# One-core decoder trunk in FP32 parts: work moved off VectorE's queue, an earlier x, wo groups dealt anew, a last expert slot by halves

## Chip, cores and metric

One core of one Trainium2 chip. The metric is the device time of one execution in microseconds; the time before is the median of three runs. A view of the profile shows one profiled execution, with times from its first instruction.

## The reference, cut to what matters

x is 256 tokens by 1024 features, float32. The trunk has two layers, each a mixer and a channel mixer, with an RMS norm ahead of each and a plain residual add behind it.

```python
for i in range(DEPTH):                       # DEPTH = 2
    u = rms_norm(h, norm_mix[i])
    mix = diff_attention(u, ...) if i == 0 else moba_attention(u, ...)   # w_qkv 1024x3072, w_o 1024x1024
    h = h + mix
    u = rms_norm(h, norm_ffn[i])
    ffn = swiglu(u, ...) if i == 0 else moe_swiglu(u, ...)               # d_ff 2816; 8 experts of 3584, top 2
    h = h + ffn
return rms_norm(h, final_norm)
```

## The kernel before, in words

Every weight passes through one pipeline. A **slot** is a weight tile of 2 MB (`ring`, seven of them); a **group** is 128x512 of it, eight to a slot. SyncE (SP) loads a slot when the slot seven ahead of it is used up. ScalarE (ACT) copies two groups at a time into `whi` (twelve groups deep, line 508, in the experts line 681): the rounded high part. VectorE (DVE) subtracts it from the slot and leaves the low part in `wlo` (line 863, two or four groups at a time; line 1123 in the experts). TensorE (PE) multiplies three times for each product: high by high, high by low, low by high (lines 1312 to 1314). Activations are split in the same way into `xhi` (ACT, line 528) and `xlo` (DVE, line 871). All order is written out by hand in four instruction streams; `split_to(n)` on ACT and `halve_to(n)` on DVE work through the groups up to n (rounded up to the piece: one group in the first slot, four in whole slots of the dense FFN, two elsewhere), and an engine that waits in one of them does nothing else.

**Start.** x comes as two halves of 128 tokens (`rowbuf`), PE turns both (line 1476), ACT and DVE split them, and PE runs slot 0. The first slot comes in pieces (`head_in`, line 450). `keep_clock` (line 1465) issues transposes whose result nobody reads; 16 stand at the start and 10 ahead of the first gather. The norm's scale isn't applied to x: squares are summed (`squares` line 518, `add_squares` line 896), PE sums columns after the second group of slot 1 (`sum_norm`, line 1337) and spreads the result after the fifth (`spread_norm`, line 1342), and q, k, v are scaled when they leave PSUM.

**Attention steps.** Each layer has 16 units (pair of heads by token block) and 18 steps. In step t PE does scores(t), weigh_values(t-2) (line 1458), the first part of FILL[t] projection groups, turn_probs(t-1) (line 1442) and the rest. The groups of FILL are what PE has to do while ACT and DVE work on the softmax. Per step DVE does `minima`, `combine` (layer 0), its halving up to 8 + FILL[t]//2 groups ahead, then `output_rows(t-2)`, then more halving; ACT does `exps`, its splitting, `copy_probT`. FILL ends the 32 qkv groups at step 10; the two slots of wo (16 groups) follow, 6 of them in steps 13 to 17. After step 11 PE turns heads 0 to 3 (line 1327), after step 16 heads 4 and 5, after the steps the last two (`turn_heads(3, 4)`). In layer 0 the turn waits for `norm_heads` (DVE line 989), which waits for GpSimd (POOL, line 814), which waits for ACT's `head_square` and that for `output_rows`. wo sums over k (features) into two halves of the output: psA is half 0, psB half 1. The second wo slot of layer 0 goes two k of half 0, two of half 1, and again; that of layer 1 goes half 0 whole, then half 1 with four groups woven (lines 1532 to 1539).

**Dense FFN.** It starts as soon as the residual add (line 890) has been split again. PE sums the norm in the first up slot, after its groups 1 and 5 (lines 1519 to 1522); DVE can scale the gate product only then.

**Router, then experts.** After wo of layer 1 DVE adds the residual (lines 890, 1162) and splits the rows (`raw_lo`, line 1128), PE makes the logits (line 1551), a chain of small steps chooses experts and gathers rows (line 1585). The expert loop runs 8 times (`extra` more are possible), 21 slots each. Down slots go by k with both halves in turn. At its end `yhi` (ACT, line 764) and `ylo` (DVE, line 1293) scale the result for the scatter, which stands in the next iteration or, behind the last one, at line 1675.

Of the kernel before, what the change touches and what calls it, by code (L numbers as in the profile page):

```python
# [26 lines left out]
ALU = mybir.AluOpType  # L27
# [3 lines left out]
P = 128  # L31
GROUP = 512
# [8 lines left out]
def trunk(nc, x, norm_mix, norm_ffn, diff_w_qkv, diff_w_o, diff_lambda, diff_subln, moba_w_qkv, moba_w_o,  # L41
# [64 lines left out]
    FILL = [3] * 10 + [2, 0, 0, 2, 1, 1, 1, 1]  # L106
# [7 lines left out]
    assert sum(FILL) == 4 * GS + 6  # L114
# [25 lines left out]
    with ExitStack() as ctx:  # L140
# [28 lines left out]
        halfneg = sb("halfneg", [P, 2 * PAIRS])  # L169
        score_min = sb("score_min", [P, 2, UNITS, 2])  # L170
# [84 lines left out]
        consts = sem("consts")  # L255
        gains_T = sem("gains_T")
# [111 lines left out]
        def half_and_k(s, g):  # L368
            if s == first_slot["wo", 0] + 1:
                return g // 2 % 2, g // 4 * 2 + g % 2  # L370
            return divmod(g, slots[s][1] // 2)

        def part_of(t, s, g, size=1):
# [6 lines left out]
            return slot[:, g * GROUP:(g + size) * GROUP].rearrange("p (g n) -> p g n", n=GROUP)  # L380

# [52 lines left out]
        def _(sp):  # L434
            sp.dma_start(rowbuf[:, 0, :], x[0, 0:P, :]).then_inc(x_in[0], 16)
            for s, (src, groups) in enumerate(slots):
# [6 lines left out]
                if s in paired:  # L443
                    dst = dst.rearrange("p (k a n) -> p k a n", a=2, n=T)
                    first = 0
                    if s == 0:
                        for j in range(3):
                            ks = slice(2 * j, 2 * j + 2)
# [45 lines left out]
        def _(act):  # L494
# [98 lines left out]
            act.dma_start(rowbuf[:, 1, :], x[0, P:T, :]).then_inc(x_in[1], 16)  # L593
            split_to(1)
            act.wait_ge(gains_set, 1)
            for q in range(KD // 2):
                normed_hi(0, q)
                split_to(2 * q + 3)
# [76 lines left out]
            def item_split(i, first, last):  # L675
                for m in range(first, last, 2):
# [4 lines left out]
                    nc.scalar.copy(hi_of(NG + m, 2), part_of(ring, NS + j, g, 2)).then_inc(hi_done, 2)  # L681
# [60 lines left out]
            with act.Fori(0, n) as i:  # L742
# [19 lines left out]
                for half in range(2):  # L762
                    act.wait_ge(group_used, used_at(i, IG - 1 + half))
# [11 lines left out]
        def _(pool):  # L775
# [28 lines left out]

            def root(norm, at):
# [13 lines left out]
            nc.gpsimd.memset(f(ylo[:, :]), 0.0).then_inc(ylo_done, 2)  # L819
            root(3, rstd[:, 0, :])  # L820
# [26 lines left out]
        def _(dve):  # L847
# [144 lines left out]
            for layer in range(2):  # L992
                for pair in range(PAIRS):
                    for i in range(2):
                        nc.vector.memset(q_scale[64 * i:64 * i + 64, layer, pair:pair + 1],
                                         -SCALE / slopes[layer][2 * pair + i])
# [5 lines left out]
            halve_to(1)  # L1002
            for q in range(KD // 2):
                normed_lo(0, q)
                halve_to(2 * q + 3)
            for layer in range(2):
# [7 lines left out]
                norm_spread(2 * layer)  # L1014
                copy_qk(layer, 0)
# [51 lines left out]
                halve_to(end - 2 + AHEAD)  # L1067
# [5 lines left out]
                halve_to(end + AHEAD - 2)  # L1073
# [7 lines left out]
                halve_to(first_group[up_slot[0] + 1])  # L1081
                norm_column(1)
                norm_diagonals(1)
                halve_to(first_group[up_slot[0] + 1] + 4)
# [613 lines left out]
```

## Time and profile before

| what | value |
| --- | --- |
| median of 3 runs | 1527.39 us (1523.25 to 1528.58) |
| profiled execution, own time | 1523.65 us |
| its span | 1521.7 us |
| PE busy | 1480.4 us, 97% |
| DVE, ACT busy | 1183.8 us, 1003.2 us |
| expert loop | from 476.1 us to 1508.8 us, about 129 us an iteration |

The own time is the span and 1.95 us around it. Idle time stands in brackets ahead of an instruction, with what ended it. PE's busy time hides that its clock may be halved; the windows give that as PEclk (1.00 is 2.4 GHz, 0.50 is 1.2 GHz).

### The profile page before, as it was taken

What the parts mean: (1) busy time and instruction counts of PE and PEld (TensorE: products, weight loads), DVE (VectorE), ACT (ScalarE), POOL (GpSimd) and SP (SyncE); (2) the same over time, 40 slices, a digit from 0 to 9 for tenths busy, and PEclk for the clock granted to TensorE, in tenths of its full rate; (3) what the DMA queues carried; (4) which work ended last, traced back from release to release, by engine and by line L of the source; (5) the groups of instructions that cost most, each with busy time, mean ns of one, the idle gap of its engine ahead of it and who ended that gap; (6) DMA issues with size and microseconds to landing.
All of it is one profiled execution on the core that took longest, in us unless ns stands there. A gap on an engine that the chain in (4) does not pass through costs nothing.

```text
span 1521.7 us, 23192 instructions
## 1 busy us (share of the span) xinstructions
PE 1480.4 (97%) x8172; PEld 1257.6 (83%) x8172; DVE 1183.8 (78%) x1176; ACT 1003.2 (66%) x1322; POOL 22.1 (1%) x50
## 2 busy tenths in 40 slices
PE   8989999999999999999999999999999999999997
PEld 8878999999887878777887787878778787778875
DVE  6776555566558888888888888888888888888887
ACT  5555444446547776777777777777777777767775
POOL 0000000000001000000000000000000000000000
PEclk9989999999999999999999999999999999999998
DMA  9833444474324999999899999989989999998981
GB/s 336 305 112 111 167 167 141 164 271 170 114 106 161 345 360 327 331 361 360 303 351 364 330 322 360 339 308 366 360 311 345 360 327 331 359 362 302 354 305 42
DMA packets 187543, 426.36 MB, mean 280 GB/s; under 512 B 4641, under 2 KB 23234, under 8 KB 187458
## 3 DMA queue, kind: packets, MB, share of 16 engines
q1 hardware_dynamic: 187104, 424.33, 77.6%
q10 hardware_dynamic: 354, 1.07, 0.2%
q8 instruction: 33, 0.54, 0.1%
q14 instruction: 52, 0.43, 0.1%
HBM read 424.33 MB, written 1.05 MB: 280 GB/s over the span
## 4 chain that ended last, share of the span: by engine, by line
PE 83%; DVE 7%; ACT 4%; issue 4%; DMA 0%; ACTq 0%; DVEq 0%; POOL 0%; POOLq 0%
PE psA L1312 9%; PE psA L1314 9%; PE psA L1313 9%; PE psB L1312 9%; PE psB L1314 9%; PE psB L1313 9%; PE psY L1312 8%; PE psY L1314 7%; PE psY L1313 7%; DVE wlo L1123 3%; PE psY L1585 2%; ACT whi L681 2%; PE psB L1612 2%; PE psY L1458 1%; DVE wlo L863 1%
## 5 line engine op out<-in xcount | busy, mean ns | idle before, releaser
L1123 DVE TENSOR_TENSOR wlo<-ring,whi 128x2048 fp32r<-128x2048 f32 x339 | 761.4, 2281 | 131.6 <-ACT whi L681 128.7
L681 ACT CAST whi<-ring 128x1024 fp32r<-128x1024 f32 x676 | 678.7, 1054 | 133.9 <-PE psY L1314 65.6
L863 DVE TENSOR_TENSOR wlo<-ring,whi 128x1024 fp32r<-128x1024 f32 (+2 forms) x104 | 152.7, 1488 | 69.4 <-ACT whi L508 68.8
L1312 PE MATMUL psB<-whi,ihi 128*128 128x512 f32 x448 | 181.6, 405 | 6.9 <-DVE wlo L1123 6.9
L1312 PE MATMUL psY<-whi,hhi 128*128 128x512 f32 x448 | 182.7, 408 | 0.0
L1312 PE MATMUL psA<-whi,ihi 128*128 128x512 f32 x448 | 177.8, 397 | 3.4 <-DVE ilo L1214 2.1
L1314 PE MATMUL psA<-whi,ilo 128*128 128x512 f32 x448 | 177.2, 396 | 0.0
L1314 PE MATMUL psB<-whi,ilo 128*128 128x512 f32 x448 | 177.1, 395 | 0.0
L1313 PE MATMUL psA<-wlo,ihi 128*128 128x512 f32 x448 | 176.9, 395 | 0.0
L1313 PE MATMUL psB<-wlo,ihi 128*128 128x512 f32 x448 | 176.9, 395 | 0.0
L1314 PE MATMUL psY<-whi,hlo 128*128 128x512 f32 x448 | 176.9, 395 | 0.0
L1313 PE MATMUL psY<-wlo,hhi 128*128 128x512 f32 x448 | 176.9, 395 | 0.0
L508 ACT CAST whi<-ring 128x1024 fp32r<-128x1024 f32 (+1 forms) x134 | 133.3, 1022 | 63.9 <-PE psY L1314 27.5
L1312 PE MATMUL psA<-xhi,whi 128*128 128x256 f32 x368 | 108.2, 294 | 4.0 <-DVE xlo L871 2.5
L693 ACT CAST hhi<-psB 128x512 fp32r<-128x512 f32 x56 | 32.9, 587 | 119.4 <-PE psB L1612 119.4
L1312 PEld LDWEIGHTS psY<-whi,hhi 128*128 128x128 f32 x448 | 84.5, 189 | 28.9 <-DVE wlo L1123 12.0
L1312 PE MATMUL psB<-xhi,whi 128*128 128x256 f32 x368 | 107.2, 291 | 0.0
L1312 PEld LDWEIGHTS psB<-whi,ihi 128*128 128x128 f32 x448 | 84.4, 188 | 27.2 <-DVE wlo L1123 9.9
L1312 PEld LDWEIGHTS psA<-whi,ihi 128*128 128x128 f32 x448 | 84.4, 188 | 26.4 <-DVE wlo L1123 4.8
L1313 PE MATMUL psA<-xlo,whi 128*128 128x256 f32 x368 | 105.9, 288 | 0.0
L1314 PE MATMUL psA<-xhi,wlo 128*128 128x256 f32 x368 | 105.9, 288 | 0.0
L1314 PE MATMUL psB<-xhi,wlo 128*128 128x256 f32 x368 | 104.5, 284 | 0.0
(277 smaller groups left out, 2294.6 us busy)
## 6 DMA issues: line engine op xcount, KB each, us to landing
ring<-in_moe_w_gate SPq DMA_DIRECT2D x57, 2048.0 KB, 7.8
ring<-in_moe_w_up SPq DMA_DIRECT2D x56, 2048.0 KB, 7.8
ring<-in_moe_w_down SPq DMA_DIRECT2D x56, 2048.0 KB, 7.7
ring<-in_ffn_w_gate SPq DMA_DIRECT2D x5, 2048.0 KB, 9.0
ring<-in_ffn_w_up SPq DMA_DIRECT2D x5, 2048.0 KB, 8.2
ring<-in_ffn_w_down SPq DMA_DIRECT2D x5, 2048.0 KB, 7.9
ring<-in_moba_w_qkv SPq DMA_DIRECT2D x8, 1024.0 KB, 7.5
ring<-in_diff_w_qkv SPq DMA_DIRECT2D x6, 1024.0 KB, 12.2
```

The source lines that it names most:

```text
L508: nc.scalar.copy(hi_of(m, size), part_of(ring, s, g, size)).then_inc(hi_done, size)
L681: nc.scalar.copy(hi_of(NG + m, 2), part_of(ring, NS + j, g, 2)).then_inc(hi_done, 2)
L693: nc.scalar.copy(hhi[:, :, place_of(c)], psB[:, 1, :].rearrange("p (b t) -> p b t", t=P)).then_inc(m_hhi, 1)
L863: nc.vector.tensor_tensor(part_of(wlo, s, g, size), part_of(ring, s, g, size), f(hi_of(m, size)), ALU.subtract).then_inc(lo_done, size)
L1123: nc.vector.tensor_tensor(part_of(wlo, NS + j, g, step), part_of(ring, NS + j, g, step), f(hi_of(NG + m, step)), ALU.subtract).then_inc(lo ...
L1312: mm(ps, xh, wh, start=start, stop=False, skip_group_check=shared)
L1313: mm(ps, xh, wl, start=False, stop=False, skip_group_check=shared)
L1314: return mm(ps, xl, wh, start=False, stop=stop, skip_group_check=shared)
L1458: ins = mm(psY[:, 3, i * wide:(i + 1) * wide], probsT[:, u % 2, i * (tb + 1) + kb, :], val[:, kb, c:c + wide], start=kb == 0, stop=kb == tb)
L1585: ins = mm(psY[:, 2 + q, (k % 4) * P:(k % 4 + 1) * P], rows_[:, tb * D + k * P:tb * D + (k + 1) * P], pick[:, tb, :], start=part == 0 and ...
L1612: ins = nc.tensor.transpose(psB[:, 1, fb * P:(fb + 1) * P], hid[:, fb * P:(fb + 1) * P], ident[:, :])
```

## The change

- x's second half is issued by SP behind the first two pieces of slot 0, no longer by ACT behind the gains. ACT and DVE split one group more ahead of each part of x. `keep_clock` adds 4 transposes behind the first half of x and 10 behind the second.
- 32 memsets of q_scale leave DVE; POOL makes q_scale (16 memsets and three operations). Five small operations ahead of the router leave DVE for POOL. DVE waits for `scales_set` in three places.
- FILL for steps 11 to 17 becomes 0, 2, 2, 2, 1, 1, 3: 11 groups of wo in place of 6. `turn_heads(3, 4)` stands right behind the steps; five groups follow it in both layers. The second wo slot of layer 1 is laid like that of layer 0.
- Between the layers' halves DVE halves less ahead of the residual add; the norm of the FFN is summed after group 0 of the up slot and spread after group 3.
- The last slot of an expert runs all k of half 0, then of half 1; `yhi` of half 0 waits for four groups less.

```diff
@@ -103,7 +103,7 @@
 STEPS = UNITS + 2
-FILL = [3] * 10 + [2, 0, 0, 2, 1, 1, 1, 1]
+FILL = [3] * 10 + [2, 0, 2, 2, 2, 1, 1, 3]
...
@@ -111,7 +111,7 @@
 assert all(filled[layer][11] == first_group[first_slot["wo", layer]] for layer in range(2))
-assert sum(FILL) == 4 * GS + 6
+assert sum(FILL) == 4 * GS + 11
...
@@ -167,6 +167,7 @@
     halfneg = sb("halfneg", [P, 2 * PAIRS])
+    second_head = sb("second_head", [P, 1])
...
@@ -253,6 +254,7 @@
     consts = sem("consts")
+    scales_set = sem("scales_set")
...
@@ -366,7 +368,7 @@
     def half_and_k(s, g):
-if s == first_slot["wo", 0] + 1:
+if s in (first_slot["wo", 0] + 1, first_slot["wo", 1] + 1):
...
@@ -378,6 +380,12 @@
+    def item_part(t, j, g, size):
+if j == IS - 1:
+    half, k = divmod(g, FBW)
+    return t[(NS + j) % RING][:, :].rearrange("p (k h n) -> p h k n", h=2, n=GROUP)[:, half, k:k + size, :]
+return part_of(t, NS + j, g, size)
...
@@ -445,6 +453,8 @@
             for j in range(3):
+                if j == 1:
+                    sp.dma_start(rowbuf[:, 1, :], x[0, P:T, :]).then_inc(x_in[1], 16)
...
@@ -590,12 +600,11 @@
 act.dma_start(gain_rows[4 * KD:4 * KD + 1, :], diff_subln[:, :]).then_inc(gains_in, 16)
-act.dma_start(rowbuf[:, 1, :], x[0, P:T, :]).then_inc(x_in[1], 16)
-split_to(1)
+split_to(2)
     normed_hi(0, q)
-    split_to(2 * q + 3)
+    split_to(2 * q + 4)
...
@@ -678,7 +687,7 @@
         act.wait_ge(group_used, used_at(i, m + 2 - HL))
-        nc.scalar.copy(hi_of(NG + m, 2), part_of(ring, NS + j, g, 2)).then_inc(hi_done, 2)
+        nc.scalar.copy(hi_of(NG + m, 2), item_part(ring, j, g, 2)).then_inc(hi_done, 2)
...
@@ -760,7 +769,7 @@
     for half in range(2):
-        act.wait_ge(group_used, used_at(i, IG - 1 + half))
+        act.wait_ge(group_used, used_at(i, IG - 4 + 4 * half))
...
@@ -801,6 +810,15 @@
+pool.wait_ge(consts, 1)
+for pair in range(PAIRS):
+    nc.gpsimd.memset(q_scale[:, 0, pair:pair + 1], -SCALE / slopes[0][2 * pair])
+    nc.gpsimd.memset(q_scale[:, 1, pair:pair + 1], -SCALE / slopes[1][2 * pair])
+link(nc.gpsimd.memset(second_head[:, :], 1.0))
+link(select(second_head[:, :], slopes[1][0] / slopes[1][1], ALU.is_gt, 64, [[0, 1]], -1))
+nc.gpsimd.tensor_tensor(q_scale[:, 1, :], q_scale[:, 1, :], repeat(second_head[:, 0], 1, PAIRS),
+                        ALU.mult).then_inc(scales_set, 1)
...
@@ -817,6 +835,12 @@
 nc.gpsimd.memset(f(ylo[:, :]), 0.0).then_inc(ylo_done, 2)
+nc.gpsimd.memset(over[:, 0:5], 0.0)
+nc.gpsimd.memset(over2[:, 0:2], 0.0)
+nc.gpsimd.memset(over4[:, 0:4], 0.0)
+nc.gpsimd.tensor_scalar(first_place[:, :], expert_no[:, :], float(P), None, ALU.mult)
+nc.gpsimd.tensor_scalar(jump_base[:, :], expert_no[:, :], -float(P), float(P * (E - 1)), ALU.mult,
+                        ALU.add).then_inc(scales_set, 1)
...
@@ -989,20 +1013,15 @@
 
-for layer in range(2):
-    for pair in range(PAIRS):
-        for i in range(2):
-            nc.vector.memset(q_scale[64 * i:64 * i + 64, layer, pair:pair + 1],
-                             -SCALE / slopes[layer][2 * pair + i])
 dve.wait_ge(gains_set, 1)
-halve_to(1)
+halve_to(2)
     normed_lo(0, q)
-    halve_to(2 * q + 3)
+    halve_to(2 * q + 4)
...
@@ -1012,6 +1031,7 @@
     norm_spread(2 * layer)
+    dve.wait_ge(scales_set, 1)
...
@@ -1064,13 +1084,12 @@
         break
-    halve_to(end - 2 + AHEAD)
+    halve_to(end + 4)
         normed_lo(2, q)
-    halve_to(end + AHEAD - 2)
...
@@ -1078,10 +1097,10 @@
     sum_squares(1)
-    halve_to(first_group[up_slot[0] + 1])
+    halve_to(first_group[up_slot[0]] + 4)
     norm_diagonals(1)
-    halve_to(first_group[up_slot[0] + 1] + 4)
+    halve_to(first_group[up_slot[0] + 1])
...
@@ -1120,7 +1139,7 @@
         dve.wait_ge(hi_done, used_at(i, m + step))
-        nc.vector.tensor_tensor(part_of(wlo, NS + j, g, step), part_of(ring, NS + j, g, step),
+        nc.vector.tensor_tensor(item_part(wlo, j, g, step), item_part(ring, j, g, step),
...
@@ -1140,14 +1159,9 @@
                         ALU.subtract).then_inc(rt_split, 1)
-nc.vector.tensor_scalar(first_place[:, :], expert_no[:, :], float(P), None, ALU.mult)
-nc.vector.tensor_scalar(jump_base[:, :], expert_no[:, :], -float(P), float(P * (E - 1)), ALU.mult, ALU.add)
-nc.vector.memset(over[:, 0:5], 0.0)
-nc.vector.memset(over2[:, 0:2], 0.0)
-link(nc.vector.memset(over4[:, 0:4], 0.0))
 
-dve.wait_ge(group_used, NG - 4)
+dve.wait_ge(group_used, NG - 2)
...
@@ -1181,6 +1195,7 @@
 norm_column(3)
+dve.wait_ge(scales_set, 2)
...
@@ -1477,6 +1492,7 @@
             ins.then_inc(turn_done, 1)
+    keep_clock(10 if tb else 4)
...
@@ -1500,8 +1516,7 @@
     end = first_group[first_slot["wo", layer] + 2]
-    last_turn = end - GS + (2 if layer == 0 else 0)
-    fill(layer, filled[layer][STEPS], last_turn)
+    last_turn = filled[layer][STEPS]
...
@@ -1516,9 +1531,9 @@
                 turned_group(up_slot[c], g, 2, psB, width[c])
-                if c == 0 and g == 1:
+                if c == 0 and g == 0:
                     sum_norm(1)
-                if c == 0 and g == 5:
+                if c == 0 and g == 3:
...
@@ -1527,16 +1542,15 @@
 
-fill(1, last_turn, end - 4)
+fill(1, last_turn, end - 2)
 for fb in range(4):
-    for k in range(4):
-        pe.wait_ge(xlo_done, 4 * ATTN[1] + 2 + k // 2 + 1)
-        ins = rows_block(end - 4 + k, fb, block_of(1, fb), xhi[:, 4 + k, :], xlo[:, 4 + k, :], False, k == 3)
+    for k in range(2):
+        ins = rows_block(end - 2 + k, fb, block_of(1, fb), xhi[:, 6 + k, :], xlo[:, 6 + k, :], False, k == 1)
     if fb == 3:
-        ins.then_inc(group_used, 4)
+        ins.then_inc(group_used, 2)
...
@@ -1620,7 +1634,7 @@
         m = GS * j + g
-        wh, wl = whi_of(NG + m), part_of(wlo, NS + j, g)[:, 0, :]
+        wh, wl = whi_of(NG + m), item_part(wlo, j, g, 1)[:, 0, :]
...
@@ -1631,7 +1645,7 @@
         if kind == "down":
-            k, half = divmod(g, 2)
+            half, k = divmod(g, FBW) if j == IS - 1 else (g % 2, g // 2)
...
```

## Rows read from the trace of the kernel before

**Rows 1.** The page: the span, and the first line of the busy times.

```profile
span 1521.7 us, 23192 instructions
...
PE 1480.4 (97%) x8172; PEld 1257.6 (83%) x8172; DVE 1183.8 (78%) x1176; ACT 1003.2 (66%) x1322; POOL 22.1 (1%) x50
```

**Rows 2.** Windows: us, busy PE, PEld, DVE, ACT, POOL (instructions), PEclk, DMA, GB/s.

```profile
10.14:16.97 6.83, 6.15 (x29) 6.18 (x30) 6.83 (x15) 5.43 (x13) 0.00 (x0) 0.50 1.06 376
...
98.90:102.31 3.41, 1.28 (x9) 0.85 (x8) 3.33 (x12) 2.64 (x9) 0.00 (x0) 1.00 0.84 265
102.31:112.55 10.24, 8.28 (x38) 6.95 (x39) 7.10 (x23) 5.21 (x16) 0.00 (x0) 0.50 0.29 117
...
122.78:126.20 3.42, 3.42 (x20) 3.41 (x18) 0.09 (x1) 1.34 (x3) 0.00 (x0) 0.50 0.00 0
126.20:142.70 16.50, 16.50 (x138) 16.29 (x137) 10.49 (x11) 7.45 (x13) 1.20 (x2) 1.00 0.37 128
```

**Rows 3.** Timeline of PE, start: start us, us, instruction, count, idle before.

```profile
8.38 1.09 PE L1476 MATMUL psY<-ident,rowbuf 128*128 128x128 f32 x8 [1.11 <-DMA rowbuf<-in_x]
10.82 0.55 PE L1312 MATMUL psA<-xhi,whi 128*128 128x256 f32 x1 [1.34 <-DVE xlo L871]
...
28.22 0.47 PE L1312 MATMUL psB<-whi,xhi 128*128 128x512 f32 x1
```

**Rows 4.** Timelines of the other engines, start.

```profile
0.83 3.08 DVE L995 MEMSET q_scale<- 64x1 f32 x32 [0.83 <-PEq L1689]
1.21 3.15 SPq L450 DMA_DIRECT2D ring<-in_diff_w_qkv  x6
...
2.28 0.36 ACTq L593 DMA_DIRECT2D rowbuf<-in_x  x1
...
18.07 1.05 ACT L508 CAST whi<-ring 128x1024 fp32r<-128x1024 f32 x1 [2.50 <-DMA ring<-in_diff_w_qkv]
19.02 2.04 ACT L601 COPY resT<-psY 128x512 f32<-128x512 f32 x4
...
26.11 3.49 DVE L863 TENSOR_TENSOR wlo<-ring,whi 128x1024 fp32r<-128x1024 f32 x3
```

**Rows 5.** Timeline of PE, layer 0: steps 11 to 16, dense FFN's start.

```profile
101.52 0.33 PE L1442 MATMUL psY<-ident,probs 128*128 128x128 f32 x1 [2.11 <-DVE probs L964]
...
106.90 0.69 PE L1442 MATMUL psY<-ident,probs 128*128 128x128 f32 x2 [0.83 <-DVE probs L964]
...
120.83 0.33 PE L1442 MATMUL psY<-ident,probs 128*128 128x128 f32 x1 [1.62 <-DVE probs L964]
121.86 0.46 PE L1458 MATMUL psY<-val,probsT 128*128 128x128 f32 x2 [0.69 <-DVE rowbuf L977]
...
143.88 0.36 PE L1312 MATMUL psA<-xhi,whi 128*128 128x256 f32 x1 [1.18 <-DVE xlo L871]
...
175.22 0.39 PE L1312 MATMUL psA<-xhi,whi 128*128 128x256 f32 x1 [1.44 <-DVE wlo L863]
```

**Rows 6.** Timeline of DVE, layer 0, steps 12 and 17 and the wo groups.

```profile
106.77 1.40 DVE L882 SCALAR_TENSOR_TENSOR xlo<-psA,gain_cols,xhi 128x512 fp32r<-128x512 f32 x2
...
130.27 0.76 DVE L989 TENSOR_TENSOR rowbuf<-rowbuf,head_rstd 128x256 f32<-128x256 f32 x2 [1.84 <-POOL head_rstd L814]
...
136.78 4.50 DVE L863 TENSOR_TENSOR wlo<-ring,whi 128x2048 fp32r<-128x2048 f32 x2 [1.20 <-ACT whi L508]
```

**Rows 7.** Waits, 413 to 450 us (layer 1): total, times, longest.

```profile
PE psY L1458 <- ACT probsT L561: 1.5, 2, 1.2
```

**Rows 8.** Timeline of DVE behind wo of layer 1.

```profile
456.14 1.29 DVE L890 TENSOR_TENSOR resT<-psA,resT 128x512 f32<-128x512 f32 x2 [0.18 <-PE psA L1314]
...
462.83 0.76 DVE L1128 TENSOR_TENSOR ilo<-resT,ihi 128x256 fp32r<-128x256 f32 x2
```

**Rows 9.** Waits of PE over the whole span: total, times, longest.

```profile
PE psB L1312 <- DVE wlo L1123: 6.9, 7, 1.4
```

**Rows 10.** The chain, at an expert iteration's end: start us, us, what.

```profile
604.44 2.64 issue
```

**Rows 11.** Timeline of PE behind the last expert.

```profile
1510.74 0.50 PE L1675 MATMUL psY<-yhi,pickT 128*128 128x512 f32 x1 [1.94 <-DVE ylo L1293]
```

## The prediction, made before the changed kernel was run

> **What bounds the kernel now.** I read the page first: PE is busy for 97% of the span [rows 1], so a part of the change counts only where PE waits, or where its clock is low. The windows come next, for the clock [rows 2]. It is at 0.50 (1.2 GHz) from 10.14 to 16.97, from 102.31 to 112.55 and from 122.78 to 126.20: 20.5 us, of which half, 10.2 us, would come back at 2.4 GHz if PE had work throughout. The timelines of PE show its waits: 1.11 and 1.34 us at the start [rows 3], 2.11, 0.83, 1.62 and 0.69 in steps 11 to 16 of layer 0, 1.18 ahead of the dense FFN and 1.44 in it [rows 5]. In the expert loop seven waits sum to 6.9 us [rows 9]. What ends nearly all of them is DVE, in the order its stream is written in, often behind a copy by ACT. So each part is judged by where it puts things in DVE's order.
>
> A group is 12 matmuls; at full clock 138 matmuls took 16.50 us [rows 2], 0.12 us each, so a group takes 1.43 us. A copy of two groups by ACT takes 1.05 us, a halving of two by DVE 1.2 us (3.49 for three) [rows 4], one of four 2.25 us (4.50 for two) [rows 6].
>
> **Costed at nothing.** The 32 memsets run from 0.83 to 3.91 [rows 4], and DVE's next work waits for gains that PE turns well after that; POOL is idle then, and the scales are wanted only after 30 us. DVE's five small operations ahead of the router sit in time that it waits for ACT anyway. If that cover were gone they would cost about 0.5 us. SP issues x at its third place: 1.21 plus two issues of 0.53 is 2.27, ACT issued it at 2.28 [rows 4]. So it isn't issued sooner; it only stands ahead of the later pieces of slot 0 in one queue. The last slot by halves: ACT gets `yhi` of half 0 earlier, but `ylo` stands behind DVE's halving for the next item, in the loop and at the end, so PE's wait of 1.94 us [rows 11] stays.
>
> **Start.** x may land between as late as now and 1.11 us sooner, where PE's wait for it ends [rows 3]. I take 0.7, nearer to the latter since x moves ahead of 1.5 MB of weights. The extra transposes fill the 1.34 us wait, so the clock should stay up: slot 0 starts at 10.2 and ends after 96 x 0.12 = 11.5 us, at 21.8; two groups of slot 1 take it to 24.6. That is over 3 us ahead, but it doesn't last. The third group needs a halving that stands behind the sum of squares on DVE: it starts at 26.11 and the first of its three pieces ends at 27.3 [rows 4]. That chain hangs on ACT, which can copy x (19.02) only after slot 1 has landed (18.07) [rows 4]; nothing here lands it sooner. So PE resumes at 27.3 where it was at 28.22 [rows 3]: **0.9 us gained**, with some 2.3 us of new idle time ahead. The clock fell behind waits of 2.11 and of 1.62 + 0.69 [rows 2, 5]; behind 1.18 and 1.44 [rows 5] no fall is seen. The new one is nearest to the first two, so I take a fall, 3.4 us long as the shortest was [rows 2], that costs 1.7: **+0.8 us**; bounds -0.9 and +0.8.
>
> **Layer 0, steps 12 to 17.** FILL gives PE work in steps 12 to 14, but each group has to be split first.
> - Step 12: PE is free at 106.07 (106.90 less 0.83 [rows 5]). Its next instruction is now the first wo group, which needs `xlo` of heads 0 to 3; DVE makes it until 108.17 [rows 6]. The softmax work that ran at 106.90 is queued behind that. Wait 2.1.
> - Steps 13 to 15: halvings now stand ahead of `output_rows`; I get waits of 0.1, 0.05 and 0.4.
> - Step 16: the halving of the last wo pair (1.2) stands ahead of `combine`, as in the case of the 1.62 wait: 1.35.
> - Step 17: its first group belongs to heads 4 and 5, turned just before: 0.9.
> - `turn_heads(3, 4)`: halving up to 9 groups ahead now reaches into the FFN, where pieces are four wide. So two copies (2.1) and a halving of four (2.25) stand ahead of `output_rows` of the last unit (0.35); from there to the end of `norm_heads` it was 2.6 (130.27 - 1.84 to 131.03 [rows 6]). With 0.4 for ACT to get there that is 7.7 us, against 0.9 and three groups, 5.2: wait 2.5. Before, five groups covered it.
>
> New waits 7.4, old ones 0.83 + 1.62 + 0.69 = 3.1: +4.3. The half clock from 122.78 goes (-1.7), and in that up to 112.55 PE has some 1.2 us less work (-0.6): **+2.0**. The last wait (2.5) is nearest to 2.11, so another fall: +1.7. Together **+3.7**; bounds: -3 (old waits go, nothing new) and +5.
>
> **Dense FFN.** The halving of four that stood ahead of the residual add moves behind it, so the wait of 1.18 goes. But there it is in front of the squares. I get 0.35 at gate group 4 and 1.2 at the first up group, whose halving follows the sum of squares: **+0.4**; bounds -1.2 and +2.25 (the whole piece uncovered). The spread comes two groups sooner, but the wait of 1.44 [rows 5] starts with PE's end of the up slot: no change.
>
> **Layer 1, steps.** No POOL chain here, and no pieces of four. Step 12 waits 1.3 for the heads, later waits (1.5 in one group [rows 7]) shrink by as much: **0**, bounds -1.5 and +1.3, with +1.7 if the clock falls.
>
> **Behind wo of layer 1.** The new layout finishes psA two groups before the end, not four. DVE's chain from psA to the last split rows took from 456.14 to 463.59, 7.45 us, nearly all busy [rows 8]. Four groups covered 5.7 of it, two cover 2.9: **+2.9**. Bounds: +1.6 (DVE's own waits for ACT inside it, 1.3, vanish) and +4.
>
> **Sum.** 0.8 + 3.7 + 0.4 + 0 + 2.9 = +7.8. On the profiled execution's own 1523.65 (span 1521.7 and 1.95 around it) that is 1531.4. It lies 3.7 below the median of the runs, 1527.39, near their fastest. For a median of new runs I take the middle between 1531.4 and 1535.2: **1533.5 us**. About 0.3% (4.6 us) is what a measurement of this kernel can tell from no change.
>
> **Rivals.**
> - *The waits are covered* (0.27). PE reaches the new groups later than I reckon, the clock stays up: -0.9 at the start, 0 in layer 0, 0.4 in the FFN, 2.9 behind wo: +2.4, some 1528. For it: half of my waits in layer 0 are under 1 us, the size of my error. Against: the 2.1 of step 12 and the 2.5 of the last turn are orders in the code.
> - *The clock* (0.10), the one that ends faster. The extra transposes and groups keep 2.4 GHz through all three stretches: -10.2, and the 2.9 behind wo stays: -7.3, 1520. It decides at two points: slot 1 mustn't wait for the squares (they would have to end by 24.6), and the wait of 2.11 in step 11, ahead of the fall at 102.31, would have to go; no group is added ahead of it.
> - *The code of the expert loop* (0.06). At an iteration's end ACT stands still for 2.64 us in "issue" [rows 10], with nothing to wait for, and then PE waits for a halving that waits for ACT; the seven waits are 6.9 us [rows 9]. DVE's and ACT's streams ahead of the loop get shorter; if that moved the code so that ACT's stop went, the sum would be +0.9, some 1528.5. Against: only one ACT instruction goes. The Trainium skill ("Runtime: NRT & Kernel Launch", Instruction fetch mechanics) says that a taken branch to a page of code that is no longer held has to wait for it to be fetched; by that rule DVE, whose code does shift, could gain such a stop as well as ACT lose one. The trace agrees in that the stop stands right at ACT's loop end.
> - *A part that doesn't do what it says*: the last slot by halves, in all cases at zero, for the reason above.
>
> **How the numbers follow.** My forecast has 0.57, its own range 1530 to 1537. Faster: the clock, 0.10. Within 0.3%: covered waits and code, 0.33. Slower: 0.57. The range takes in the covered waits (1528 less 3 for the spread of runs) and, above, a fall in layer 1 (+1.7) and one behind wo (+1): 1525 to 1539.
>
> **What would show it.** Right: slot 1's third group waits for DVE near 24.6 to 27.3 and the clock is 0.50 right behind; in layer 0 PE waits about 2 us for `xlo` ahead of the first wo group and 2.5 ahead of the last turn; from PE's last wo group to the last row split it is 4.6 us, not 1.8. Wrong: if the last turn doesn't wait, or if PE's waits per expert iteration (about 1 us) change, in either direction; the second would outweigh all else here.

## The result, and the profile after

The changed kernel takes **1538.05 us** (median of 4 runs, 1537.45 to 1540.89), the kernel before beside it 1526.63: ratio **1.0081**, 95% interval 1.0058 to 1.0103: slower by 11.4 us in the medians, by 12.4 in the ratio. The prediction was 1533.5 with 1525 to 1539, and slower as the likeliest case; the measured time lies 1 us inside the upper end. The profiled execution is the slowest of the four (1540.89); so its span lies 17.4 us over that of before [rows 1], while the medians lie 11.4 apart. The page of the changed kernel begins:

```profile
span 1539.1 us, 23210 instructions
...
PE 1490.5 (97%) x8186; PEld 1260.6 (82%) x8186; DVE 1182.6 (77%) x1139; ACT 1002.7 (65%) x1322; POOL 23.4 (2%) x74
```

PE is busy 10 us longer though its program is nearly the same. The busy share says nothing about it; the clock in the windows does (us, busy PE, PEld, DVE, ACT, POOL with instructions, PEclk, DMA, GB/s):

```profile
10.00:14.00 4.00, 3.75 (x31) 3.69 (x31) 4.00 (x9) 4.00 (x11) 0.00 (x0) 1.00 1.07 375
...
29.43:32.85 3.42, 3.42 (x10) 2.64 (x9) 2.58 (x6) 2.38 (x3) 0.72 (x1) 0.50 1.06 381
...
104.53:114.77 10.24, 6.94 (x32) 6.23 (x33) 5.36 (x15) 4.07 (x12) 0.00 (x0) 0.50 0.29 116
...
473.17:483.00 9.83, 9.83 (x50) 9.37 (x47) 5.82 (x27) 6.71 (x10) 3.50 (x10) 0.50 0.10 35
483.00:493.65 10.65, 10.65 (x38) 9.39 (x38) 7.18 (x21) 6.57 (x15) 2.65 (x6) 0.50 0.01 2
```

Slot 0 now runs at 2.4 GHz from its start, and the falls of before at 10.14 and 122.78 [rows 2] are gone. In their place stand 3.41 us at 29.43 and 20.48 us, from 473.17 to 493.65, where before had none. The timeline of PE shows what stands ahead of each, and PE's other waits (start us, us, instruction, count, idle before):

```profile
27.38 0.61 PE L1352 MATMUL psY<-ones,hidT 128*128 128x1 f32 x4 [2.54 <-DVE hidT L926]
28.52 0.50 PE L1327 MATMUL psB<-whi,xhi 128*128 128x512 f32 x1 [0.53 <-DVE wlo L887]
...
110.50 0.55 PE L1327 MATMUL psA<-xhi,whi 128*128 128x256 f32 x1 [2.25 <-DVE xlo L906]
...
130.40 0.44 PE L1457 MATMUL psY<-ident,probs 128*128 128x128 f32 x2 [1.12 <-DVE probs L988]
132.93 0.36 PE L1327 MATMUL psA<-xhi,whi 128*128 128x256 f32 x1 [0.92 <-DVE xlo L906]
...
139.48 0.66 PE L1342 MATMUL psY<-ident,rowbuf 128*128 128x128 f32 x4 [2.01 <-DVE rowbuf L1013]
...
153.81 0.38 PE L1327 MATMUL psA<-xhi,whi 128*128 128x256 f32 x1 [0.18 <-DVE wlo L887]
160.87 0.39 PE L1327 MATMUL psB<-xhi,whi 128*128 128x256 f32 x1 [1.06 <-DVE wlo L887]
...
471.09 0.29 PE L1565 MATMUL psA<-ihi,rt_parts 128*16 128x256 f32 x1 [2.44 <-DVE ilo L1147]
...
472.32 0.29 PE L1565 MATMUL psA<-ihi,rt_parts 128*16 128x256 f32 x1 [0.59 <-DVE ilo L1147]
...
1528.21 0.50 PE L1689 MATMUL psY<-yhi,pickT 128*128 128x512 f32 x1 [1.92 <-DVE ylo L1308]
```

These are the orders that the prediction read out of DVE's stream: the sum of squares ahead of the third group of slot 1, the heads ahead of the first wo group (2.25, [rows 5] had 0.83 there), `norm_heads` ahead of the last turn (2.01), the split rows ahead of the logits (2.44 and 0.59), and `ylo` at the end as before (1.92, [rows 11]). The 1.18 ahead of the FFN [rows 5] is gone.

Landmarks by stage, from the traces of all kernels (us; the fifth number is from the last logits product to the end of the first expert iteration; "half" is how long the clock was at 0.50, leaving out the tail behind the experts). The kernels of the lower part are told below.

| kernel | scores(0) | to first FFN down | layer 1: scores(0) to logits | logits | to end of iteration 1 | half |
| --- | --- | --- | --- | --- | --- | --- |
| before | 39.9 | 152.7 | 99.4 | 2.1 | 136.2 | 20.5 |
| changed | 41.9 | 156.2 | 100.3 | 5.3 | 142.1 | 34.1 |
| changed, second trace | 43.3 | 156.4 | 102.8 | 5.4 | 138.1 | 37.6 |
| changed_tile_last | 42.6 | 156.4 | 100.4 | 5.3 | 139.4 | 27.3 |
| logits_filled | 41.0 | 155.9 | 100.3 | 5.3 | 136.4 | 13.7 |
| start_only | 41.9 | 152.7 | 99.1 | 2.1 | 138.7 | 23.9 |
| start_x_on_act | 43.5 | 151.7 | 102.2 | 2.1 | 137.8 | 27.3 |
| fill_layer0_only | 38.8 | 154.8 | 102.4 | 2.1 | 137.9 | 27.3 |
| l1_tail_only | 38.4 | 152.9 | 99.3 | 5.0 | 139.0 | 23.9 |
| one_tile_more | 39.1 | 151.7 | 102.4 | 2.1 | 138.1 | 23.9 |
| parts_left | 38.9 | 153.3 | 99.4 | 2.1 | 136.2 | 13.7 |
| squares_ahead_of_slot1 | 37.4 | 152.2 | 102.4 | 2.1 | 137.8 | 23.9 |
| filled_waits | 37.2 | 151.6 | 99.4 | 2.1 | 137.7 | 10.2 |
| filled_waits_2 | 38.0 | 148.7 | 99.3 | 2.1 | 136.3 | 0 |

### The profile page after: what moved, and what is told of

The parts are those of the page before. It is cut to its first block, busy times and chain, and to the rows that moved or that the text cites. A ratio compares the mean times of both kernels' runs of the same rounds, so it can differ in the third digit from the quotient of the medians.

```text
span 1539.1 us, 23210 instructions
## 1 busy us (share of the span) xinstructions
PE 1490.5 (97%) x8186; PEld 1260.6 (82%) x8186; DVE 1182.6 (77%) x1139; ACT 1002.7 (65%) x1322; POOL 23.4 (2%) x74
## 4 chain that ended last, share of the span: by engine, by line
PE 81%; DVE 7%; ACT 5%; issue 5%; DMA 1%; SPq 0%; ACTq 0%; POOL 0%; DVEq 0%; POOLq 0%
PE psB L1327 9%; PE psA L1327 9%; PE psB L1329 9%; PE psB L1328 9%; PE psA L1329 8%; PE psA L1328 8%; PE psY L1327 7%; PE psY L1329 7%; PE psY L1328 7%; DVE wlo L1142 3%; PE psY L1599 2%; ACT whi L690 2%; PE psB L1626 2%; DVE wlo L887 1%; ACT whi L518 1%
## 5 line engine op out<-in xcount | busy, mean ns | idle before, releaser
L690 ACT CAST whi<-ring 128x1024 fp32r<-128x1024 f32 x676 | 678.5, 1054 | 136.4 <-PE psY L1329 66.2
L887 DVE TENSOR_TENSOR wlo<-ring,whi 128x1024 fp32r<-128x1024 f32 (+2 forms) x104 | 152.9, 1489 | 66.3 <-ACT whi L518 65.9
L1328 PE MATMUL psB<-xlo,whi 128*128 128x256 f32 x368 | 104.0, 283 | 0.0
```

The source lines that it names most:

```text
L690: nc.scalar.copy(hi_of(NG + m, 2), item_part(ring, j, g, 2)).then_inc(hi_done, 2)
L887: nc.vector.tensor_tensor(part_of(wlo, s, g, size), part_of(ring, s, g, size), f(hi_of(m, size)), ALU.subtract).then_inc(lo_done, size)
L1328: mm(ps, xh, wl, start=False, stop=False, skip_group_check=shared)
```

## The experiments

Some of the kernels have one part of the change each, some the whole change with one thing altered, and some are new versions of the kernel before. There are eleven, and the changed kernel ran a second time; the twelve ran on four chips, each beside the kernel before (medians 1525.18 to 1527.19).

**The changed kernel again,** for a second trace. I expected 1537 to 1539, with a fall of the clock of 10 to 20 us behind the logits. Measured: 1537.70 against 1525.18, ratio 1.0078 (1.0063 to 1.0093). Behind the logits the clock was at 0.50 for 3.41 and 6.83 us (from 475.09 and 485.33). It was also at 0.50 for 6.83 in layer 1's steps and 3.41 in the experts, where the first trace had none.

**The end of wo of layer 1 alone.**

```diff
-            if s == first_slot["wo", 0] + 1:
+            if s in (first_slot["wo", 0] + 1, first_slot["wo", 1] + 1):
...
-            dve.wait_ge(group_used, NG - 4)
+            dve.wait_ge(group_used, NG - 2)
...
-            fill(1, last_turn, end - 4)
+            fill(1, last_turn, end - 2)
```

> The kernel before with only the new end of wo of layer 1: its second slot is laid two k of half 0, two of half 1, and again, DVE adds the residual from two groups before the end (not four), and the merged loop has two k. In the trace of the changed kernel the clock is at 0.50 from 473.17 to 493.65, behind waits of 2.44 and 0.59 us in the logits. Theory: the layout alone makes this wait and the fall. Then PE waits 2 to 3 us in the logits, the clock is 0.50 for 13 to 21 us behind it, the experts' first group comes 8 to 12 us later than before, and the time is 1535 to 1539 us. Rival (the fall needs what lies ahead of it, the other waits of layer 1): the wait is there, but no fall, and the time is +2.9, 1529 to 1531.

Measured: 1528.94 against 1526.11, ratio 1.0025 (1.0014 to 1.0035). The wait is there, and behind it a fall. Timeline of PE, then windows:

```profile
463.69 0.29 PE L1550 MATMUL psA<-ihi,rt_parts 128*16 128x256 f32 x1 [2.23 <-DVE ilo L1128]
464.93 0.29 PE L1550 MATMUL psA<-ihi,rt_parts 128*16 128x256 f32 x1 [0.59 <-DVE ilo L1128]
```

```profile
467.00:473.50 6.50, 5.43 (x49) 5.08 (x48) 4.98 (x23) 6.34 (x9) 3.72 (x10) 1.00 0.09 33
473.50:483.74 10.24, 9.48 (x31) 8.04 (x31) 8.09 (x22) 7.10 (x15) 2.63 (x6) 0.50 0.01 2
```

The logits take 5.0 us in place of 2.1: +2.9, the number of the prediction. But the clock stays up for 8.6 us behind the wait and falls then, in the gathers. Both theories have a half: the price of the wait is the rival's, the fall is my theory's, though not where it put it, and the time (+2.8) is just under what both had.

**The logits' wait filled, in the changed kernel.**

```diff
             for k in range(KD):
+                if k in (4, 6):
+                    keep_clock(20 if k == 4 else 4, psY[:, 3, T + P:2 * T])
                 pe.wait_ge(tlo_done, k + 1)
```

> The kernel after with 20 transposes that nobody reads ahead of PE's wait for the fifth logits block and 4 ahead of the seventh, in a bank that is free there. They take about 0.12 us each at full clock, 2.4 + 0.5, as much as the waits of 2.44 and 0.59. Theory: the half clock from 473.17 to 493.65 comes from these idle times; it goes, and with it 7 to 10 us: 1528 to 1531. Rival: the clock is set by how little PE does in the chain of small steps behind the logits as well; then it falls all the same, within 10 us behind the logits, and the time is 1536 to 1538.

Measured: 1534.45, ratio 1.0066 (1.0040 to 1.0092) against the same kernel before. The transposes take the place of the wait, and the clock is 1.00 through the logits, the chooser and the gathers:

```profile
467.40 2.34 PE L1480 MATMUL psY<-ident 128*128 128x128 f32 x20
470.00 0.29 PE L1567 MATMUL psA<-ihi,rt_parts 128*16 128x256 f32 x1 [0.25 <-DVE ilo L1147]
```

```profile
472.00:480.00 8.00, 6.91 (x60) 6.30 (x58) 6.31 (x27) 6.70 (x10) 3.87 (x11) 1.00 0.14 51
480.00:490.00 10.00, 8.18 (x43) 6.71 (x42) 8.63 (x22) 8.00 (x16) 2.22 (x5) 1.00 0.00 0
```

From the last logits product to the end of the first iteration it is 136.4 us, against 142.1, 138.1 and 139.4 in the three traces of the change with the wait: 1.7 to 5.7 us less, not the 7 to 10 that I expected from the one trace I had. In the medians it is 3.6, in the ratios 0.12 to 0.15%, with intervals that overlap.

**FILL and the last turn in layer 0 alone.**

```diff
-    FILL = [3] * 10 + [2, 0, 0, 2, 1, 1, 1, 1]
+    FILL = [[3] * 10 + [2, 0, 2, 2, 2, 1, 1, 3], [3] * 10 + [2, 0, 0, 2, 1, 1, 1, 1]]
...
-                last_turn = end - GS + (2 if layer == 0 else 0)
+                last_turn = end - GS if layer else filled[layer][STEPS]
```

> The kernel before with the new FILL (0, 2, 2, 2, 1, 1, 3 from step 11) and the new place of the last turn in layer 0 alone. The prediction had +2.0 for the waits, and +1.7 for a fall of the clock behind the last turn. The trace of the changed kernel has no fall there. Theory: from before scores(0) to the first down group of the FFN it is +1.5 to +3, of which most lies at the last turn (a wait of about 2 us), and the time is 1528 to 1531. Rival: with the other parts of the change away, the clock falls behind the last turn as I had assumed: +3.7.

Measured: 1529.44, ratio 1.0021 (1.0012 to 1.0031). From scores(0) to the first down group 154.8 us, +2.1. PE's waits:

```profile
107.10 0.55 PE L1311 MATMUL psA<-xhi,whi 128*128 128x256 f32 x1 [2.25 <-DVE xlo L881]
...
127.52 0.44 PE L1441 MATMUL psY<-ident,probs 128*128 128x128 f32 x2 [1.10 <-DVE probs L963]
130.05 0.55 PE L1311 MATMUL psA<-xhi,whi 128*128 128x256 f32 x1 [0.92 <-DVE xlo L881]
136.60 0.66 PE L1326 MATMUL psY<-ident,rowbuf 128*128 128x128 f32 x4 [0.69 <-DVE rowbuf L988]
```

Here the clock was at 0.50 from 129.62 to 133.03, ahead of the last turn and not behind it. PE came later to a wait whose end DVE sets, and so waited 0.69 and not 2.01: here a fall ahead of a wait cost less than half its length, since the wait took most of it up. The rival's fall behind the last turn was in none of the five traces with this FILL.

**The start alone,** and with x on ACT's queue again.

```diff
+                            if j == 1:
+                                sp.dma_start(rowbuf[:, 1, :], x[0, P:T, :]).then_inc(x_in[1], 16)
...
-                split_to(2 * q + 3)
+                split_to(2 * q + 4)
...
+                keep_clock(10 if tb else 4)
```

> The kernel before with only the changed start: x's second half issued by SP, one group more split ahead of each part of x, 4 and 10 more transposes. Theory: slot 0 runs at full clock from about 10.3, the third group of slot 1 waits about 2.5 us for DVE, the clock falls to 0.50 behind that for 3.4 us, and scores(0) comes between +0.8 (my sum) and +2.0 (what the changed kernel's trace shows) later than before; 1528 to 1530. Rival: the +2.0 of the changed kernel comes from the POOL operations or the wait on them, which are away here; then scores(0) is within 0.5 us of the place of before.

> The changed start alone, but x's second half is issued by ACT as before. With the whole new start, slot 1's landing let ACT go on at 19.25, with first group at 10.37; in a kernel with the old start at 17.37, with first group at 10.17. Theory: x in SP's queue, ahead of five pieces of the weights, pushes the landing of slot 1 back by 1 to 1.9 us, and with it the squares and the third group of slot 1. With x back on ACT slot 1 lands as before, the wait for the squares is 0.6 to 1.3 us in place of 2.55, and scores(0) comes 1 to 2 us sooner than with the new start, at 39.9 to 40.9. Rival: the landing differs between executions whatever the queue; then it stays near 19 and scores(0) at 41.9.

Measured: 1527.65, ratio 1.0016 (1.0003 to 1.0028), scores(0) at 41.9; with x on ACT 1525.19, ratio 1.0000 (0.9990 to 1.0010), scores(0) at 43.5. My theory of the queue fell in the trace: slot 1 lands late with x on either queue (timeline of ACT, x on ACT; [rows 4] had 18.07):

```profile
19.61 1.05 ACT L508 CAST whi<-ring 128x1024 fp32r<-128x1024 f32 x1 [4.32 <-DMA ring<-in_diff_w_qkv]
```

That trace is of the slowest of its kernel's ten runs (1529.71), so it may overstate the cost. Whether x on SP costs anything, the two overlapping intervals leave open.

**The squares ahead of slot 1,** an order of my own on the kernel before.

```diff
-                split_to(2 * q + 3)
+                split_to(min(2 * q + 3, GS))
...
                     squares(3 * layer, q)
+                    if layer == 0 and q == 1:
+                        split_to(GS + 2)
```

> The kernel before with another order at the start: ACT copies x and squares half of it before it splits the first two groups of slot 1, DVE adds the first square before it halves them. The chain to the sum of squares no longer starts with the landing of slot 1. Theory: PE's waits ahead of the third group of slot 1 (0.9 to 2.5 us in all the traces so far) go, the third group starts at 2.9 us from the end of slot 0, and scores(0) comes 1 to 1.5 us sooner than with the order of before: 37 to 38.7; total -1. Rival: ACT's split of slot 1's first groups comes later than PE wants it, and what is won in front of the third group is lost in front of the first.

DVE's side is cut in the same way (halving to 8, and of two more behind the first add). Measured: 1524.83 against 1525.18, ratio 0.9997 (0.9987 to 1.0006). PE doesn't wait ahead of the third group of slot 1, which starts at 25.7 (28.2 before, [rows 3]), and scores(0) comes at 37.4, 2.5 us sooner than in the trace of before and 1.0 to 1.6 sooner than in the other traces with the old start. The total doesn't show it: in this trace the clock fell at 426.27 and at 477.47 for 10.2 us together, where the trace of before had none.

**One tile more, unused.** Outside PE's waits, an expert iteration took 128.34 and 128.35 us in the changed kernel's and `logits_filled`'s traces, and 128.05 to 128.08 in those of the seven kernels without the whole change that had run by then.

```diff
         halfneg = sb("halfneg", [P, 2 * PAIRS])
+        unused = sb("unused", [P, 1])
```

> The kernel before with one tile more, a single number per partition, unused, declared where the change declares second_head. Three traces with the whole change have PE's expert iterations at 128.35 us without their waits, seven traces without it at 128.05 to 128.08, and the difference is spread over the whole iteration. The new tile moves all tiles behind it by 32 bytes in each partition (ihi from 205056 to 205088, hhi, hlo, ilo, q_hi, k_hi with it), so that they no longer begin at a multiple of 64. Theory: that slows PE's reading of them; then this kernel has 128.3 to 128.4 per iteration without waits, and 2 to 3 us more in all, 1527.5 to 1529 beside 1525 to 1526. Rival: it is the code or the order of the last slot; then it is 128.05 to 128.08 and the time that of before.

> The whole change, but second_head is declared behind all other tiles, so that it moves none; nothing else differs. Before with one tile more had 128.33 us per expert iteration without waits, the parts left with second_head last 128.04. Theory: the iterations come to 128.05, the total 2 to 3 us under the changed kernel's, 1534.5 to 1536 where before is at 1525 to 1526.5; the waits (2.25 ahead of the first wo group, 2.0 at the last turn, 2.44 in the logits) stay, with a fall of 3 to 20 us behind the last. Rival: in the changed kernel the 0.28 per iteration has another cause as well, then it stays above 128.2.

Measured: `one_tile_more` 1527.13, ratio 1.0007 (0.9997 to 1.0017); the change with `second_head` as the last tile 1538.71 against 1527.19, ratio 1.0076 (1.0063 to 1.0089). The totals don't tell it, the traces do. Windows over iterations 3 to 8: before, one tile more, changed, changed with the tile last:

```profile
729.14:1504.53 775.39, 768.49 (x3494) 619.52 (x3494) 660.64 (x451) 567.22 (x648) 0.00 (x0) 1.00 0.91 330
```

```profile
732.20:1509.72 777.52, 770.02 (x3494) 617.79 (x3494) 660.69 (x451) 567.33 (x648) 0.00 (x0) 1.00 0.91 329
```

```profile
745.00:1522.00 777.00, 770.00 (x3494) 617.81 (x3493) 660.91 (x451) 566.49 (x648) 0.00 (x0) 1.00 0.90 329
```

```profile
743.09:1518.56 775.47, 768.41 (x3494) 618.93 (x3494) 660.90 (x451) 566.60 (x648) 0.00 (x0) 1.00 0.91 330
```

The same 3494 matmuls at the same clock keep PE busy for 768.49 and 768.41 us where the tiles begin as before, and for 770.02 and 770.00 where one tile of a number has pushed them by 32 bytes. That is 1.5 us in six iterations, 2 in eight. In iteration length without waits it is 128.33 with the tile and 128.06 in the change without its push. Both kernels differ from their partner in nothing but that tile. The other traces agree: in iterations 3 to 8 the mean without waits is 128.33 to 128.35 in all four traces where the tile pushes the others, and 128.04 to 128.09 in the other ten.

**The parts left:** operations from DVE to POOL, the FFN's orders, the last slot by halves, on the kernel before, with `second_head` last.

```diff
-                halve_to(end - 2 + AHEAD)
+                halve_to(end + 4)
...
-                        k, half = divmod(g, 2)
+                        half, k = divmod(g, FBW) if j == IS - 1 else (g % 2, g // 2)
```

> The parts of the change not tried so far, on the kernel before: the operations moved from DVE to POOL, the FFN's new orders, the last slot by halves; with second_head declared behind all other tiles, so that it moves none. Layer 1's end, FILL and the start are as before. Theory: each is worth little. Expert iterations 128.05 to 128.08 us without waits; the wait of 1.18 ahead of the FFN goes and 1.2 comes at the first up group, so the first down group is within 0.6 of before, counted from scores(12); PE's last wait stays 1.94; the total within 1 us of before. Rival: the iterations are at 128.35 as in the changed kernel, so the last slot or the code is the cause and not the tile's place; then +2 to 3 us.

Measured: 1526.80, ratio 1.0007 (0.9996 to 1.0018). scores(12) to the first down group +0.4, iterations 128.04 without waits, the last wait 1.94.

**Waits filled with transposes,** on the kernel before, first and second version. Both also have the squares ahead of slot 1, and the change's 4 and 10 transposes behind x. The cut shows the second; the first has {11: 16, 12: 6, 16: 12} and nothing in layer 1.

```diff
+                        if layer == 0:
+                            keep_clock({11: 18, 12: 4, 15: 13}.get(t, 0), psY[:, 2, T + P:2 * T])
                         turn_probs(layer, t - 1)
...
+                    if layer == 1 and t == 12:
+                        pe.wait_ge(qk_raw, 2 * (4 * layer + 3) + 2)
+                        keep_clock(9)
                     if t < UNITS:
                         scores(layer, t)
```

> The kernel before with that order of the start, the 4 and 10 transposes behind x, 16, 6 and 12 transposes ahead of the turns of probabilities in steps 11, 12 and 16 of layer 0 (in the bank that these turns use), and 16 ahead of the last scatter. Nothing else of the change. Theory: the clock falls behind idle time of PE of about 2 us and stays up where transposes run in its place; then the half clock of before (6.83, 10.24 and 3.41 us in layer 0, and some of the tail) goes, and the time is 10 to 12 us less: 1514 to 1517. Rival: the clock goes by how much PE does in the steps with no groups; then it falls in steps 11 to 14 all the same, the gain is 2 to 4 us, and the time is 1522 to 1524.

> The kernel with filled waits, with the transposes better placed: 18 in step 11 and 4 in step 12 ahead of the turns of probabilities, 9 ahead of the turn of heads in step 11, 13 in step 15 (12 stood in step 16, too late for the wait of 1.62), in layer 1 nine ahead of scores(12), 18 in place of 10 ahead of the first gather, 16 ahead of the experts. Its first trace still had falls of 3.41 us at 117.10 and 6.83 at 468.67. Theory: both go, and those that other traces show at 427 to 437, and the time is 2 to 5 us under that of the kernel with filled waits: 1516 to 1519. Rival: transposes also put work behind them late; then the falls go and the time stays at 1521.

Measured: 1521.16 against 1525.18, ratio **0.9977** (0.9968 to 0.9986), then 1518.20 against 1526.23, ratio **0.9954** (0.9940 to 0.9969). Of the first, its rival's time came nearer than mine (4 us gained, 10 to 12 expected): the fall of step 11 was gone, but one at 117.10 stayed behind a wait of 1.62, where I had the step wrong by one, and one at 468.67. In the second the clock is at 1.00 from 10.68, where its record begins in this trace, to 1509.13, where PE has all but finished:

```profile
10.68:500.00 489.32, 478.17 (x3698) 450.35 (x3697) 318.48 (x549) 262.48 (x469) 16.43 (x28) 1.00 0.52 182
500.00:1509.00 1009.00, 998.34 (x4546) 804.06 (x4544) 859.00 (x590) 737.85 (x850) 1.00 (x3) 1.00 0.91 330
1509.13:1515.50 6.37, 0.00 (x0) 0.00 (x0) 2.54 (x2) 0.00 (x0) 1.79 (x3) 0.50 0.41 165
```

It beats both kernels. Its six runs lie within 3 us (1517.3 to 1520.3), the 23 of before on the same chip within 6.7.

## Why the prediction was right, and where it was not

**The direction and the range held;** the sum was +7.8, measured +11.4. (The middle of 1531.4 and 1535.2 is 1533.3, not 1533.5; and by that same middle the rival on code would be at 1526.4 and the clock at 1518.2, where I gave 1528.5 and 1520.) The parts, each alone, give in ratios 16 (start), 21 (layer 0), 25 (behind wo of layer 1), 7 (the tile) and 7 (the parts left) hundredths of a per cent: 0.76%, 11.6 us, about what was measured (0.76 to 0.81% in three comparisons). Each single ratio has an interval of 1.5 to 2 us either way, and layer 1's new FILL, +1.0 in the traces, ran in none of them, so that the sum fits so well is partly luck. The parts as read from traces come to some 15 us, more than the medians show; the gap is open, though in both measurements of the changed kernel the profiled execution was the slowest of four.

- *Start, forecast +0.8.* Right in kind: 2.54 us for DVE's squares, the clock at 0.50 for 3.41 from 2 us behind that wait, slot 0 at full clock. The term that failed is the 0.9 us gained: the third group starts at 28.52, 0.3 later than the 28.22 of before, not at 27.3. With the 1.7 of the half clock, as I had it, that is the +2.0 of this trace. In the trace of before scores(0) is at 39.9; the four others with the old start have 38.4 to 39.1, the six with the new one 41.0 to 43.5. So traces show about +3.4, totals +2.4 (1.0016) and 0 (x on ACT). Two things were missing: the half clock at 10.14, which is part of why before reached its third group only at 28.22, is 6.83 us in that trace and 0 to 3.41 in the others; and "nothing here lands it sooner" should have allowed for later: slot 1's last packet lands at 18.3 to 19.5, at 17.3 to 18.1 in the eight kernels that don't split one group further.
- *Layer 0 and FFN, forecast +3.7 and +0.4.* Measured 3.2 to 3.8 from scores(0) to the first down group. The waits came nearly as worked out (forecast 2.1, 1.35, 0.9, 2.5, FFN 0.35 and 1.2; measured 2.25, 1.12, 0.92, 2.01, 0.18, 1.06). The fall that I had assumed behind the last turn (+1.7) never came, and still the total was nearly met: that is luck. What it made up for is that the clock gave back less than the 2.3 us of the sum (1.7 and 0.6). Windows over this stretch, before and changed (the first numbers: its length, PE's busy time):

```profile
39.90:192.60 152.70, 141.31 (x1080) 131.96 (x1080) 99.39 (x209) 82.08 (x183) 6.82 (x9) 0.96 0.47 169
```

```profile
41.90:198.10 156.20, 140.51 (x1080) 130.36 (x1080) 99.65 (x209) 82.06 (x183) 6.82 (x9) 0.97 0.44 160
```

  PE is idle for 11.39 and 15.69 us, +4.3, near the 4.7 of the sum, but busy for only 0.8 less, with 3.41 us of half clock gone: that term was mis-sized. `fill_layer0_only` is at +2.1, which meets my +2.0 without the fall by luck too: it has as much half clock as before and a wait of 0.69 in place of 2.5. FFN alone: +0.4.
- *Layer 1, steps, forecast 0.* +1.0 in three traces of four, inside its bounds (+1.3). The wait of step 12 is 1.41 and the later ones shrank by less: PE's idle time grew by 0.4. The other 0.5 is in its busy time, of an unknown cause.
- *Behind wo of layer 1, forecast +2.9.* +3.1 in the logits (5.29 against 2.15), +2.9 alone: the best term. What was mis-sized is its clock, "+1" at most: the three traces of the change have falls of 20.48, 10.24 and 3.41 + 6.83 us between the logits and the first experts, worth 1.9 to 5.9 us against the trace of before (136.2 in the table). But of the other eight traces with the old end six have 1.5 to 2.5 there too. So the trace of before was a lucky draw: the means are 139.9 us in the three and 137.4 in the nine with the old end, and the change adds rather 2 than 6.
- *Experts, forecast 0.* The seven waits are 7.8 us against 6.9 [rows 9], ACT's stops at the loop's end 2.4 to 3.3 us, of the kind of [rows 10]: the rival on code fell. But 0.28 us per iteration came from where I looked at nothing, the address of the tiles.
- *Last slot by halves, memsets:* nothing, as forecast.
- *The rival that ends faster,* the clock, had about the right worth, if somewhat much (-10.2), and was wrong that the change would bring it: `filled_waits_2` gains 7 to 8 us with the clock up throughout, by filling the waits of the kernel before.

The working fits a median better than a profiled execution: I set the sum against one trace's falls as if they belonged to the kernel. The table shows that they don't. With the same waits of 1.10 and 0.42 us in layer 1, some executions have a fall of 6.83 behind them (102.4 us) and others none (99.4). The Trainium skill ("TensorE: Matmul & The Clock Gate", Part 1: The HAM clock gate) says that the gate's bookkeeping doesn't start with the kernel, so that the same kernel differs between runs. These traces agree in that the falls differ, in the changed kernel's two (34.1 and 37.6 us in all) as well; none shows that this is why. The 0.3% was too wide as the limit of what totals tell: with ten runs, 0.16 to 0.25% were told from no change in three kernels. But three of the others have an interval that holds 1 though their trace shows a cause.

## What to carry to other kernels

Where a wait of about 2 us stands on PE and PE bounds the kernel, count twice: the wait, and the chance of a clock fall behind it. Fill it with work that nobody reads in a bank that is free, sized from the trace; with one reordering that was worth 0.5% here, where the reordering alone was worth nothing that a total shows. And before a reordering is judged, take several traces of the old kernel, and see that no declaration has moved the tiles that the matmuls read.

## What the runs showed of the hardware that I had not expected

- **Where a tile begins.** With `ihi`, `ilo`, `hhi` and `hlo` 32 bytes off a multiple of 64, PE needs 0.2% more for the same matmuls (770.0 against 768.4 us). In these windows PE's weight loads are busy 617.8 us against 618.9 to 619.5, so the loads aren't longer. Which operand is slower wasn't tried, nor any other offset.
- **The clock can stay low while PE is busy.** From 473.17 to 493.65 it was at 0.50 with PE busy for all 20.48 us by its records (whose ends are modelled), most of it small transposes and the gathers' 128-column products. No run isolated why.
- **Code arrives over the same DMA engines.** In the changed kernel's DMA view of 16 to 20 us one packet of 16 KB of instructions stands among slot 1's, whose share of 16 engines makes it 1.15 us long:

```profile
q1 hardware_dynamic: 2123, 1.24, 110.8%
q8 instruction: 1, 0.02, 1.8%
```

  The view of before has no such line there. All six traces with the new start have that packet between 16.57 and 17.18, and slot 1's last packet at 18.3 to 19.5; the kernels with the old start have it at 18.7 or later, or not at all ahead of 20, and 17.3 to 18.1. I take it for PE's code: PE gets sooner to its next stretch when slot 0 runs at full clock. Against a simple cause: the two kernels with filled waits have the packet at 17.15 and 17.40, and slot 1 at 18.03 and 18.11. So it stays a suspicion.
